# PSUM banks exchanged and a gated product moved in a hybrid attention and state-space block

## What is computed

```python
h = rmsnorm(x, norm_g)
proj = h @ w_in                      # q | K, V | gates | gate_nsa (gn) | u | gate_s5 (gs) | merge gates
# attention: 8 heads in 2 groups; compressed keys, and two branches (selected blocks, window) with rotary q and k
o_nsa = g0 * o_cmp + g1 * o_sel + g2 * o_win
branch_a = (o_nsa * silu(gate_nsa)) @ w_proj_nsa
# state space: y = scan(u); z = gelu(y)
branch_b = (z * sigmoid(z @ w_glu + b_glu) * silu(gate_s5)) @ w_proj_s5
merged = sigmoid(mg_a) * branch_a + sigmoid(mg_b) * branch_b
out = rmsnorm(x + merged @ w_out, final_g)
```

## Time and profile before

| what | value |
|---|---|
| median of 3 runs (lowest to highest) | 439.96 us (439.51 to 440.15) |
| the profiled execution: time | 439.65 us |
| the profiled execution: span, first to last instruction | 437.9 us |
| granted PE clock, mean | 0.991 |
| busy: PE, DVE, ACT, POOL | 417.7, 283.0, 200.8, 170.5 us |
| chain that ended last | PE 62%, DVE 22%, ACT 6% |

### The profile page before, as it was taken

The page is one execution under the profiler, slowest core; times in us unless marked ns, Lnnn a source line. Parts: engine busy times, 40 slices in busy tenths (PEclk is TensorE's granted clock), DMA queues, the critical chain, the costliest instruction groups (busy, mean ns, idle before and its releaser), DMA issues.

```text
span 437.9 us, 7316 instructions
## 1 busy us (share of the span) xinstructions
PE 417.7 (95%) x2768; PEld 339.7 (78%) x2768; DVE 283.0 (65%) x641; ACT 200.8 (46%) x394; POOL 170.5 (39%) x93
## 2 busy tenths in 40 slices
PE   5898999999999999969999999999999999999994
PEld 5686888898778777737777778888888888888994
DVE  3779997899999998987898952071071171170544
ACT  6744577824234667696467432222222222231433
POOL 0354242443369501244241354454454454454430
PEclk9999999999999999979999999999999999999999
DMA  8996946534841254100101113934333333333105
GB/s 286 146 250 175 164 144 191 159 82 123 257 96 49 49 99 145 49 1 3 48 4 47 49 49 103 330 80 110 99 86 106 97 88 104 98 96 97 48 1 192
DMA packets 71746, 48.19 MB, mean 110 GB/s; under 512 B 20368, under 2 KB 67104, under 8 KB 71712
## 3 DMA queue, kind: packets, MB, share of 16 engines
q1 hardware_dynamic: 71408, 47.39, 41.7%
q10 hardware_dynamic: 304, 0.33, 0.2%
HBM read 43.20 MB, written 4.19 MB: 108 GB/s over the span
## 4 chain that ended last, share of the span: by engine, by line
PE 62%; DVE 22%; ACT 6%; SPq 3%; issue 3%; DMA 2%; POOL 1%; POOLq 1%; DVEq 0%; ACTq 0%
PE bank L1063 17%; PE bank L1065 16%; PE bank L1064 16%; DVE bank L1471 5%; DVE X L1471 5%; PE bank L1366 4%; PE bank L1345 3%; PE bank L1327 3%; DMA raw<-in_w_in 2%; DVE s5p L1471 1%; PE bank L1358 1%; ACT w_hi L786 1%; ACT z L1006 1%; DVE X L1691 1%; DVE prob L1815 1%
## 5 line engine op out<-in xcount | busy, mean ns | idle before, releaser
L737 POOL TENSOR_TENSOR w_lo<-raw,w_hi 128x1024 fp32r<-128x1024 f32 (+3 forms) x56 | 134.3, 2398 | 192.5 <-ACT w_hi L786 160.0
L1063 PE MATMUL bank<-hT_lo,w_hi 128*128 128x512 f32 x288 | 115.0, 399 | 2.9 <-DVE CT L1601 1.8
L1065 PE MATMUL bank<-hT_hi,w_hi 128*128 128x512 f32 x288 | 112.3, 390 | 0.0
L1064 PE MATMUL bank<-hT_hi,w_lo 128*128 128x512 f32 x288 | 112.2, 390 | 0.0
L786 ACT ACTIVATE w_hi<-raw 128x1024 fp32r<-128x1024 f32 (+2 forms) x56 | 58.4, 1043 | 72.9 <-PE bank L1065 71.9
L1063 PEld LDWEIGHTS bank<-hT_lo,w_hi 128*128 128x128 f32 x288 | 54.1, 188 | 16.5 <-issue 5.7
L1065 PEld LDWEIGHTS bank<-hT_hi,w_hi 128*128 128x128 f32 x288 | 54.1, 188 | 11.5
L1064 PEld LDWEIGHTS bank<-hT_hi,w_lo 128*128 128x128 f32 x288 | 54.1, 188 | 10.4
L993 ACT ACTIVATE prob<-prob,nmax 128x128 f32<-128x128 f32 (+2 forms) x64 | 35.3, 553 | 25.3 <-DVE nmax L1815 25.3
L1022 ACT ACTIVATE tmp<-bank 128x512 f32<-128x512 f32 x16 | 9.6, 597 | 59.6 <-PE bank L1065 57.2
L1884 DVE SCALAR_TENSOR_TENSOR tmp<-tmp,bank 128x512 f32<-128x512 f32 x8 | 5.5, 688 | 44.6 <-ACT tmp L1022 44.6
(11 more groups left out here) (252 smaller groups left out, 766.4 us busy)
## 6 DMA issues: line engine op xcount, KB each, us to landing
raw<-in_w_in SPq DMA_DIRECT2D x28, 512.0 KB, 3.8
raw<-in_w_in SPq DMA_DIRECT2D x16, 256.0 KB, 3.8
raw<-in_w_out SPq DMA_DIRECT2D x8, 512.0 KB, 3.7
x_sb<-in_x SPq DMA_DIRECT2D x4, 512.0 KB, 5.0
raw<-in_w_proj_s SPq DMA_DIRECT2D x4, 512.0 KB, 3.5
raw<-in_w_proj_nsa SPq DMA_DIRECT2D x8, 256.0 KB, 3.9
r_sb<-in_x SPq DMA_DIRECT2D x1, 2048.0 KB, 8.7
out<-r_sb SPq DMA_DIRECT2D x7, 256.0 KB, 2.3
```

The source lines that it names most:

```text
L737: nc.gpsimd.tensor_tensor(lo, whole, hi.bitcast(F32), ALU.subtract).then_inc(lo_done, 1)
L1063: nc.tensor.matmul(dst, w[0], x[1], start=first, stop=False, skip_group_check=True)
L1064: nc.tensor.matmul(dst, w[1], x[0], start=False, stop=False, skip_group_check=True)
L1065: return nc.tensor.matmul(dst, w[0], x[0], start=False, stop=last, skip_group_check=True)
```

## The change

Three edits, none of which adds or removes an instruction.

1. Banks 0 and 3, and 1 and 4, change places for q0 to q3, WT0 to WT3, S0 to S7, kwi, kc and V0 to V3.
2. Y0 to Y7 use the banks 0, 5, 6, 7, 2, 3, 6, 7 in place of 0, 5, 6, 7 twice.
3. `gate_pair(0)` goes from the head of step 10 into step 9, ahead of `normalise(8)`; the fill job gn2 is spread over steps 6 to 10, with 1, 2, 1, 2, 2 pieces. `pair_high(0)` stays in step 10.

```diff
-FILL = dict(gn1=(0, 4), gn2=(6, 9), glu0=(12, 13), glu1=(15, 16), gn3=(18, 20), glu2=(22, 23), glu3=(24, 25),
+FILL = dict(gn1=(0, 4), gn2=(6, 10), glu0=(12, 13), glu1=(15, 16), gn3=(18, 20), glu2=(22, 23), glu3=(24, 25),
...
-    use("q0", 3, 2)
-    use("q1", 4, 2)
-    use("WT0", 0)
-    use("WT1", 1)
+    use("q0", 0, 2)
+    use("q1", 1, 2)
+    use("WT0", 3)
+    use("WT1", 4)
...
-    for i, b in enumerate((0, 1, 3, 4)):
+    for i, b in enumerate((3, 4, 0, 1)):
         use(f"V{i}", b, 2)
...
-        use(f"Y{m}", (0, 5, 6, 7)[m % 4])
+        use(f"Y{m}", (0, 5, 6, 7, 2, 3, 6, 7)[m])
...
-                if pair_ends:
+                if pair_ends and s > 10:
                     gate_pair((s - 10) // 6)
...
+                if s == 9:
+                    gate_pair(0)
                 if 1 <= s <= NS:
                     normalise(s - 1)
```

More of the change, by code:

```diff
@@ L158, in bank_plan @@
     use("u3", 1)
-    use("q0", 3, 2)
-    use("q1", 4, 2)
-    use("WT0", 0)
-    use("WT1", 1)
+    use("q0", 0, 2)
+    use("q1", 1, 2)
+    use("WT0", 3)
+    use("WT1", 4)
     use("q2", 2, 2)
-    use("WT2", 0)
-    use("WT3", 1)
+    use("WT2", 3)
+    use("WT3", 4)
     use("KR", 6)
-    use("q3", 3, 2)
-    for m, b in enumerate((4, 0, 1, 2)):
+    use("q3", 0, 2)
+    for m, b in enumerate((1, 3, 4, 2)):
         use(f"S{m}", b, 1 + m % 2)
     use("ksl", 6)
-    for m, b in enumerate((4, 0, 1, 2)):
+    for m, b in enumerate((1, 3, 4, 2)):
         use(f"S{4 + m}", b, 1 + m % 2)
-    use("kwi", 3)
-    use("kc", 4, 8)
+    use("kwi", 0)
+    use("kc", 1, 8)
     use("vc", 2, 8)
-    for i, b in enumerate((0, 1, 3, 4)):
+    for i, b in enumerate((3, 4, 0, 1)):
         use(f"V{i}", b, 2)
```

## The result

The changed kernel takes 442.19 us (median of 4 runs, 441.99 to 442.95); the kernel before takes 439.74 us over 4 runs, one more than in the table ahead of the change. The ratio is 1.0062, with a 95% interval of 1.005 to 1.0074: slower by 2.5 us, clear of noise. The span of the profiled execution is 440.6 us, 2.7 more than before, at a mean clock of 0.988 (0.991 before).

What follows compares the result with a forecast made beforehand. PE was taken as the bound, busy 417.7 of 437.9 us. To 439.65 us came +0.6 at scores(12), −0.1 by edit 1 and +2.1 for the slow clock: 442.2 us, with an 8-in-10 range of 440.0 to 444.0.

Steps and rivals of the forecast that it cites:

- Edit 1, 0.1 us, and edit 2, nothing: PE's waits at q0 and Y4 only move, to W and to masked(0) before scores(2): 0.1 us gained, then nothing.
- Edit 3, up to scores(12): Early gated product removes PE's 4.16 us stall at O1 and its slow clock; PE reaches scores(12) 4.8 us sooner.
- What is late next: At scores(12) PE waits 5.4 us for POOL's low part of pair 2's queries, behind ACT's late gn3 split.
- The blocked cast: DVE's cast L1801 waits for POOL's z_lo on the shared port and ends at 194.22; masked(10) only 0.6 us sooner.
- The clock, 2.08 us: The long wait at scores(12) halves PE's clock behind it, costing 2.08 us as the old stall did.
- The sum: Over the whole kernel: +0.6 at scores(12), −0.1 by edit 1, +2.1 slow clock; together +2.6, 442.2 us.
- the low part that holds PE less: Rival at scores(12): normalise(9), not gn3's high part, releases L693, which ends at 197.9; 437.9 us, chance 0.10.
- The rival in which the new stall costs no clock: Rival at scores(12): the wait leaves PE's clock full; 440.2 us, or 439.6 without the blocked cast; chance 0.14.
- the moved stall of edit 1 costs clock: Rival ahead of W: PE's 1.5 us idling there slows its clock, up to 2 us before q3; 444.2 us, chance 0.07.

Runs made afterwards that it cites:

- e12: The changed kernel once more, unaltered, timed beside the filler run on the same chip: 442.4 us, ratio 1.0065 to the kernel before.
- e8: The kernel before, with only the queries of pair 2 (high and low part) made early: 439.56 us, ratio 1.0002.
- e5: The changed kernel, with L693 on POOL ahead of its wait for gn3's high part and not waiting for normalise(9) either: 438.5 us, ratio 0.998.
- e1: The kernel before with edits 1 and 2 alone, gated product and gn2 as before: 439.05 us against 439.42, ratio 0.9998.
- e4: The changed kernel, with L693 on POOL ahead of its wait for gn3's high part, still waiting for normalise(9): 440.06 us, ratio 1.0014.
- e11: The changed kernel, with 40 transposes of the identity on PE as filler ahead of scores(12): 440.01 us, ratio 1.0013 to the kernel before.
- e3: The changed kernel, but with the gated product left in step 10 (gn2 over steps 6 to 10): 440.15 us, ratio 1.0021.
- e7: The changed kernel, with both halves of pair 2's queries made early and gn2 in steps 6 to 9: 437.13 us, ratio 0.9945.
- e6: The changed kernel, with both halves of pair 2's queries made early on ACT and POOL: 439.1 us, ratio 0.9985.
- e10: As e7, with query_hi(3) on ACT in step 11 instead of step 10: 437.13 us, ratio 0.9943 to the kernel before.
- e2: The changed kernel, but with gn2 left in steps 6 to 9: 440.18 us, ratio 1.0025 to the kernel before.

## Why the prediction was right

The forecast was 442.2 us and slower; 442.19 was measured. That the two agree to 0.01 us is luck: single executions lie between 441.99 and 442.95, e12 gave 442.4, and the terms were off by up to 0.2 us each way. The mechanism was the one forecast. By its steps:

- **Edit 1, 0.1 us, and edit 2, nothing.** Right. The stall of q0 moved to L1100 (1.6 us where 1.5 was foreseen), and scores(2) started at 157.98, held by `masked(0)`. That start is 0.2 us earlier than before, and q3 (61.77) too, where the text had both within 0.1: DVE's own writes of W ended 0.2 us sooner (L1608 to 52.19 and not 52.38) in that execution. This shift is not a part of the change. In e8, which has the banks of before, the last of these writes starts at 51.05 as in the changed kernel, and in e5, which has the new ones, at 51.32. From the end of these writes to scores(2) it is 105.8 us in the profiles of before, of the changed kernel and of e1. e1_banks gives the two edits together 0.9998 (0.9988 to 1.0007), so the 0.1 us is not told from nothing.
- **Edit 3, up to scores(12).** Right: O1 at 189.72 (189.8), values of step 7 done at 194.6 (194.7), with a wait of 0.58 us for `copy_probs(7)`. The whole gain of 4.8 us was there for that long.
- **What is late next.** Right in each link, a little early: `masked(10)` at 193.91 (194.14), the exponentials at 194.58 (194.80), the split done at 198.38 (198.6), L693 done at 199.73 (200.0), scores(12) at 199.98 (200.1). e4 and e5 show by experiment that the start follows L693, and L693 the split of gn3. PE waited 5.36 us (5.4).
- **The blocked cast.** L1801 started at 192.75, beside z_lo, and took 1.25 us. The four executions of this line in the changed kernel (duration in ns, least, median and most) are

```profile
L1801 DVE CAST oT_hi<-tmp x4: 417/1530/2342, 192.7 to 264.7; 128x512 fp32r<-128x512 f32 x4
```

so alone it takes 0.42 us (at 220.21, with POOL idle), and here it waited 0.8. That is why `masked(10)` gained only 0.6 us, besides the 0.2 by which all was earlier. The trace agrees with the rule of the Trainium skill that the prediction named (page "SBUF — State Buffer", section "SBUF: two separate sides"), that of POOL and DVE the one that starts first has the shared port pair for its whole instruction and the other is blocked. No run took the cast away from z_lo, so the 0.8 us is read from a row. That work of POOL makes DVE's wait was seen when it was moved: the 1.87 instead of 1.00 us of L1838 in e5.
- **The clock, 2.08 us.** Right in kind, 2.25 us in size. The size was read from one event, and it varies: behind long waits PE lost 2.08 us in the profile of before, 2.25 in the changed kernel, 1.8 in e12 and 2.7 in e4, within the 1.5 to 3.1 that the text allowed. e11 tests it: same start of scores(12), no slow clock, 2.4 us less.
- **The sum.** +0.45 at scores(12) and +2.25 behind it are 2.70 us, the difference of the two spans (440.6 − 437.9). The text had +0.6 and +2.1, and −0.1 for edit 1.

Of the rivals, the low part that holds PE less was built as e4, where it gives 440.06 and not 437.9: the profiled execution shows the clock down after 3.3 us of waiting, which I had thought it might survive. One execution of e4 took 438.19 us at a mean clock of 0.999; so the rival's time exists, in one of twelve executions. The rival in which the new stall costs no clock had the right price, 440.2: e11, where filler keeps the clock up, takes 440.01. That the moved stall of edit 1 costs clock was not seen in any profile.

## What to carry to other kernels

Before a stall is removed, read what each engine's next wait would be, and follow the semaphores of the step behind it through every engine's own order. Here a fill job that ends one step later took a weight split with it, and a low part queued behind that split came 1.2 us later, while the matrix engine had come to need it 5 us sooner. A long idle stretch of PE has a price of its own: the clock behind it. Here waits of 1.6 to 1.8 us that stood alone had no such price, and those of 3.2 to 5.4 us in the attention steps brought the clock down in every profile (in e3 a later wait hid the price). It is the long gap that is to be broken up. Work that fills it (e11), or several gaps under a microsecond (e7), cost less; gaps of 0.6, 0.6, 0.7 and 1.45 us behind each other (e6) still brought the clock down in most executions.

## What was not expected of the hardware

The mean clock differs from execution to execution of the same kernel, and the time goes with it. The 23 runs of the kernel before beside e8 and e10 to e12 have three levels: 11 at 0.994 or 0.995 take 438.8 to 439.4 us, 9 at 0.991 take 439.5 to 440.1, 3 at 0.988 take 440.2 to 440.3. The changed kernel had 0.988 or 0.989 in all five runs of e12 (and 0.991 in one of the four of the result, its fastest with 441.99 us), and e7 0.995 to 0.998 in all five. So part of what one gains by breaking up a gap is that every execution, not only some, keeps its clock.

Two profiles show where such a difference comes from. In e8, whose PE works here as in the kernel before, PE is idle from 189.05 and waits the same 4.16 us for O1. The granted clock falls at about 192.2 there, and at about 190.8 in the profile of before. From O1 to scores(12) PE then takes 200.13 − 193.21 = 6.92 us in e8, and 199.53 − 193.24 = 6.29 before, where a full clock would take 4.21 (one pair later, 217.26 to 221.47). So the same wait costs 2.7 or 2.1 us of slow work by when the clock falls. Not all of the mean is such a cost: it falls once more in the last 1 to 4 us of every profile, where PE has no work left.

A fall can follow waits that are all shorter than 3 us. In e2, with waits of 0.73, 0.68, 0.97 and 2.72 us, none as long as that of e4, the clock fell only after PE had taken up its work again, at 198.44:

```profile
199.00:200.00 1.00, 1.00 (x8) 0.67 (x5) 0.54 (x2) 0.06 (x1) 0.32 (x1) 0.72 0.06 16
200.00:201.00 1.00, 1.00 (x7) 1.00 (x5) 0.57 (x1) 0.00 (x0) 0.95 (x1) 0.50 0.00 0
...
202.00:203.00 1.00, 1.00 (x4) 0.80 (x3) 0.96 (x5) 1.00 (x3) 0.00 (x0) 0.57 0.00 0
```

It stayed there for some 3 us with PE fully busy. In e6 it fell within a wait of 1.45 us, the longest there. e5 had waits of 0.6, 1.98 and 0.59 us at the same place and kept 1.00 in its profile, while nine of its twelve executions had mean clocks of 0.991 to 0.995. What decides it is not settled here.
